# Two attentions by pairs: GpSimdE scales the probabilities, VectorE only inverts their sums

## What is computed

```python
# block 1, branch a (8 heads) and branch b (8 heads on 2 key heads)
ya = moba_attention(qa, ka, heads(av, A_HEADS))
yb = nsa_attention(qb, kc, vc, ks, vs, kw, vw, gb)
#   per head: p = masked_softmax(s, mask); o = gate * (p @ v)   (selected and window parts)
merged = g[:, :, 0] * (ya @ w_up_a) + g[:, :, 1] * (yb @ w_up_b)
x = x + merged @ w_out
# block 2, layer 0
scores = einsum('bkgqd,bksd->bkgqs', q_blk, kt)
p = softmax(scores, axis=-1)
x = x + (p @ v) @ w_o
```

## Time and profile before

| | us |
|---|---|
| median of 3 runs | 1788.64 |
| lowest, highest | 1788.61, 1788.73 |
| the profiled execution | 1788.58 |
| its span | 1786.80 |
| granted TensorE clock, share of full | 0.999 |

### The profile page before, as it was taken

How to read it: one execution, slowest core, us unless ns; L and a number is a source line. 1 busy time by engine, 2 the same in 40 slices (tenths; PEclk the granted TensorE clock), 3 DMA queues, 4 the chain that set the end, 5 groups by cost and what they waited for, 6 DMA issues and landing times.

```text
span 1786.8 us, 30696 instructions
## 1 busy us (share of the span) xinstructions
PE 1752.3 (98%) x10764; PEld 1546.5 (87%) x10764; DVE 1345.2 (75%) x2466; ACT 980.0 (55%) x1679; POOL 500.1 (28%) x245
## 2 busy tenths in 40 slices
PE   8998999999999999999999999999999999999998
PEld 7995899899888888888888888877999988989997
DVE  6757849899767777777777777876579965669974
ACT  5567555479444444444444444666565545556553
POOL 0150166379144444444444444000000000000000
PEclk9999999999999999999999999999999999999999
DMA  7660454601555555555556665644455564535562
GB/s 293 203 232 13 155 189 153 224 25 48 169 185 188 188 190 190 191 191 192 189 193 226 232 223 188 242 142 165 143 193 188 188 196 149 177 129 178 189 196 75
DMA packets 84719, 313.70 MB, mean 176 GB/s; under 512 B 9360, under 2 KB 9488, under 8 KB 83216
## 3 DMA queue, kind: packets, MB, share of 16 engines
q1 hardware_dynamic: 82912, 304.44, 50.4%
q10 hardware_dynamic: 1712, 7.97, 1.3%
HBM read 304.77 MB, written 7.60 MB: 175 GB/s over the span
## 4 chain that ended last, share of the span: by engine, by line
PE 52%; issue 25%; ACT 9%; DVE 7%; DMA 3%; POOL 1%; PEld 1%; ACTq 1%; DVEq 0%; SPq 0%; POOLq 0%; PEldq 0%
PE bank L798 47%; ACT wsplit L1757 6%; PE bank L1249 3%; DMA raw<-expert_u 3%; DVE act_e L2353 2%; DVE wsplit L2347 2%; POOL wsplit L1400 1%; ACT projq L1579 1%; ACT probs L1579 0%; PEld bank L1249 0%; PE bank L843 0%; PE bank L832 0%; DVE wsplit L1891 0%; DVE projq L2106 0%; DVE att L2092 0%
## 5 line engine op out<-in xcount | busy, mean ns | idle before, releaser
L798 PE MATMUL bank<-HT,wsplit 128*128 128x256 f32 (+1 forms) x5056 | 720.0, 301 | 1.3 <-DVE HT L1934 0.9
L798 PEld LDWEIGHTS bank<-HT,wsplit 128*128 128x128 f32 x5056 | 679.3, 189 | 46.5 <-issue 2.6
L1431 POOL TENSOR_TENSOR wsplit<-raw,wsplit 128x1024 fp32r<-128x1024 f32 x111 | 289.6, 2609 | 370.6 <-ACT wsplit L1757 370.6
L2347 DVE TENSOR_TENSOR wsplit<-raw,wsplit 128x1024 fp32r<-128x1024 f32 x127 | 326.3, 2569 | 64.4 <-ACT wsplit L1757 64.3
L798 PE MATMUL bank<-wsplit,wexp 128*128 128x512 f32 x1536 | 373.4, 393 | 0.7 <-DVE wexp L2372 0.6
L798 PEld LDWEIGHTS bank<-wsplit,wexp 128*128 128x128 f32 x1536 | 279.4, 188 | 58.2 <-DVE wsplit L2347 1.9
L1757 ACT ACTIVATE wsplit<-raw 128x1024 fp32r<-128x1024 f32 x238 | 238.3, 1046 | 30.0 <-PE bank L798 26.8
L1765 ACT ACTIVATE act_e<-act_e 128x256 f32<-128x256 f32 x112 | 46.8, 418 | 317.6 <-DVE act_e L2353 317.6
L1466 ACT ACTIVATE wsplit<-raw 128x1024 fp32r<-128x1024 f32 x148 | 156.4, 1059 | 111.5 <-PE bank L798 110.5
L1891 DVE TENSOR_TENSOR wsplit<-raw,wsplit 128x1024 fp32r<-128x1024 f32 x124 | 154.5, 1258 | 78.5 <-ACT wsplit L1466 77.7
L1891 DVE TENSOR_TENSOR wsplit<-raw1b,wsplit 128x1024 fp32r<-128x1024 f32 x102 | 122.6, 1221 | 43.9 <-ACT wsplit L1466 43.5
(11 more groups left out here) (288 smaller groups left out, 2032.9 us busy)
## 6 DMA issues: line engine op xcount, KB each, us to landing
raw<-weights SPq DMA_DIRECT2D x148, 512.0 KB, 4.2
raw<-expert_v SPq DMA_DIRECT2D x127, 512.0 KB, 3.7
raw<-expert_u SPq DMA_DIRECT2D x119, 512.0 KB, 4.4
raw1b<-weights SPq DMA_DIRECT2D x102, 512.0 KB, 4.3
raw1a<-weights SPq DMA_DIRECT2D x48, 512.0 KB, 4.7
early_u<-expert_u SPq DMA_DIRECT2D x5, 512.0 KB, 3.6
raw1a<-expert_u SPq DMA_DIRECT2D x4, 512.0 KB, 3.8
parked<-memT SPq DMA_DIRECT2D x1, 2048.0 KB, 7.3
```

The costliest lines, as they stand in the source:

```text
L798: ins = pe.matmul(out, lhsT, rhs, start=start, stop=stop, **kw)
L1431: pool.tensor_tensor(wsplit[:, s, 1, :], raw0[:, s, :], f32(wsplit[:, s, 0, :]), ALU.subtract).then_inc(u_lo, 1)
L2347: dve.tensor_tensor(wsplit[:, 2 + s, 1, :], src, f32(wsplit[:, 2 + s, 0, :]), ALU.subtract).then_inc(v_lo, 1)
```

## The change

`normalise` is taken from VectorE. There, `invert` makes the inverse and signals a new semaphore `s_inv`; VectorE no longer waits for it. GpSimdE gets a `normalise(use)` that goes through all jobs in order, waits for `s_inv` of the job, makes the same two multiplications in place, and signals `s_prob` as before. It stands in GpSimdE's stream twice: for "ab" after the low part of unit 49, with the last turn of the loop over weight units written out and the units 51, 53 and 55 behind it; for "self" at the very end, after the experts.

```diff
@@ gpsimd
-            with pool.Fori(WIN_END // RAW, OUT0 // RAW) as i:
+            with pool.Fori(WIN_END // RAW, OUT0 // RAW - 1) as i:
                 lo_turn(i, WIN_END, odd)
 
+            def normalise(use):
+
+                jobs, _, Pb, _ = USES[use]
+                for j, job in enumerate(jobs, JOBS[use]):
+                    pool.wait_ge(s_inv, j + 1)
+                    for t in range(T):
+                        r, p = att[:, 2, j % 4, t:t + 1], Pb[:, j % 4, t, 0:seen(use, t)]
+                        if job["gate"] is None:
+                            ins = pool.tensor_scalar(p, p, r, None, ALU.mult)
+                        else:
+                            ins = pool.tensor_scalar(p, p, r, job["gate"](t), ALU.mult, ALU.mult)
+                    ins.then_inc(s_prob, 1)
+
+            lo_turn(OUT0 // RAW - 1, WIN_END, odd[0:1])
+            pool.wait_ge(gate3_done, 1)
+            normalise("ab")
+            lo_turn(OUT0 // RAW - 1, WIN_END, odd[1:])
...
                     pool.wait_ge(u_hi, i * 2 + (s + 1))
                     u_second_part(s)
+            normalise("self")
@@ vector
-                def normalise(step, i):
-
-                    job, j = jobs[2 * step + i], j0 + 2 * step + i
+                def invert(step, i):
+
+                    j = j0 + 2 * step + i
                     dve.wait_ge(s_exp, j + 1)
-                    link(dve.reciprocal(att[:, 2, j % 4, :], att[:, 1, j % 4, :]))
-                    for t in range(T):
-                        r, p = att[:, 2, j % 4, t:t + 1], Pb[:, j % 4, t, 0:seen(use, t)]
-                        if job["gate"] is None:
-                            ins = dve.tensor_scalar(p, p, r, None, ALU.mult)
-                        else:
-                            ins = dve.tensor_scalar(p, p, r, job["gate"](t), ALU.mult, ALU.mult)
-                    ins.then_inc(s_prob, 1)
+                    dve.reciprocal(att[:, 2, j % 4, :], att[:, 1, j % 4, :]).then_inc(s_inv, 1)
...
-                            normalise(step, i)
+                            invert(step, i)
```

More of the change, by code:

```diff
@@ L443, in block_stack @@
         s_full, s_max, s_exp, s_prob = sem("scores_full"), sem("scores_max"), sem("scores_exp"), sem("scores_prob")
+        s_inv = sem("scores_sum_inverted")
         last_gate_full, last_gate_out = sem("last_gate_full"), sem("last_gate_out")
```

## The result

The changed kernel takes **1794.61 us** (median, 1793.84 to 1797.08) against 1788.61 us of the kernel before beside it: ratio **1.0035**, 95% interval 1.0025 to 1.0045, so 6.0 us slower. The forecast was 1801.5 us (+12.9). The sign and the range held; the forecast change was twice the measured one. The profiled execution has a span of 1792.1 us against 1786.8.

A forecast was written before the change was run, and what follows sets the result against it. It took a ScalarE-VectorE latency loop to bound both attentions, with GpSimdE becoming the bound after the change: 1788.58 + 5.0 ("ab") + 7.9 ("self") = 1801.5 us, range 1780 to 1835.

The forecast's parts named there:

- What bounds the kernel before: Attentions "ab" and "self": no engine full, a ScalarE-VectorE latency loop of 3.35 and 3.98 us per pair.
- Rival 1: Both attentions: GpSimdE keeps up, turns shrink to about 2.9 and 3.5 us, gain 6.8 us, 1781.8 us; chance 0.27.
- The price of L1426: GpSimdE's comparison and product, 128 columns: 1.333 us includes a wait for VectorE; 0.84 us is its own work.
- Rival 2: GpSimdE's scalings: L1426's 1.33 us is all own work, "ab" +28.6, "self" +23.6, 1840.8 us; chance 0.13.
- one price for all forms: GpSimdE's scalings: 0.84 us for 128 columns and 1.12 for 256, with one scalar as with two.
- the term +5.0: "ab": 47.0 us of GpSimdE scalings against a 43.0 us stage, last scaling at 188.6 instead of 183.6.
- the sum by throughput: Both attentions: GpSimdE's summed scaling time, 47.0 and 35.8 us, exceeds the stages' 43.0 and 28.1 and sets their ends.
- I add nothing for hunger: GpSimdE in the attentions: four probability buffers let exponentials run two pairs ahead, so no idle time was added.
- The term +7.9: "self": 35.8 us of GpSimdE scalings from 1192.5, ending at 1228.3 instead of 1220.4.
- What would show it: New profile: GpSimdE scalings back to back, almost no idle time; "ab" near 48 us, "self" near 36.
- The odd weight units: Three units queued behind GpSimdE's 48 "ab" scalings: no cost, since GpSimdE is free by 188.6; they started at 192.91 before.
- No switch of routine: Rival 4, before GpSimdE's first scaling: it must switch routine, costing 0 to some us, inside the range.

The follow-up runs named there:

- With two products: The changed kernel with every one-product GpSimdE scaling given a second product by 1.0; 1786.01 us, ratio 0.9981.
- the shared kernel: All GpSimdE scalings written as two products, and VectorE scales each head's first tile, GpSimdE the second; 1784.87 us, ratio 0.9976.

## Why the prediction was right or wrong

- **What bounds the kernel before** was read rightly: a loop of latencies in both stages. With two products the turn of "self" came to 3.63 us where I had 3.5; in "ab" it stayed at 3.39 where I had 2.9. Rival 1's time of 1781.8 was missed mostly for that reason, and not by its price: with prices no higher than its own the kernel takes 1786.0.
- **The price of L1426** of before without its wait, 0.84 us: 0.80 alone, against 1.333 in the row. Rival 2 (1.33 as own work) was rightly put aside.
- **The step that failed first: one price for all forms**, "the same 1.12 us with one scalar" and 0.84 and 1.12 for two. Measured 0.60 and 0.92 for one, 0.45 and 0.56 for two. "ab" needs 8 x (0.60+0.92) + 16 x (0.45+0.56) = 28.3 us of GpSimdE, not 47.0, and the term +5.0 measured +0.05. That it came out so even is luck: GpSimdE was not the bound there, but a loop through it took 6.81 us for two pairs where the exchange of VectorE and ScalarE had taken 6.71. "self" needs 28.9 us, not 35.8. Rival 1 had the two-product price almost exactly (0.46 and 0.74 against 0.45 and 0.56) for the reason it gave, that the comparison is what costs. The page "GPSIMD Engine Reference" of the Trainium skill (section "Engine selection") has one figure for work with one input, roughly line rate. Here the form with two products takes 0.8 ns for each further column and that with one product 2.5, so it cannot hold for both.
- **The step that failed second: the sum by throughput.** "It becomes the bound in both": in neither. With the right price the same sum gives "self" an end at 1192.5+28.9=1221.4, +1.0, and it came 5.5 later: 4.5 us that the sum had at nothing ("I add nothing for hunger"). GpSimdE's gaps between the pairs add up to 5.0 us, and its first scaling began 0.55 sooner. I had said that four buffers feed GpSimdE two pairs ahead; but TensorE issues the scores of a later pair behind the turning that waits for GpSimdE, so no backlog forms after the first two pairs. The term +7.9 is thus +5.5 by two errors of opposite sign: the price 6.9 us too high, the waiting 4.5 us too low. That it looks close is luck.
- **What would show it**: TensorE's turning waits for GpSimdE, as forecast; "almost no idle time before the scalings" was wrong (1.09 and 0.53 us in "self", up to 4.37 in "ab").
- **The odd weight units** cost nothing: L1401 at 192.96, before at 192.91. **No switch of routine** shows before the first scaling (141.58, right behind the weight unit that ends at 141.5). **Both stages in full**: +5.5 at the last scaling of "self", +5.3 in the span. The hop is not 0.04 but 0.08 us (the chain's 1213.31 to 1213.39), once in a loop of 8.85 us, so it is small.

## What to carry to other kernels

Price an instruction by its exact form (operations, scalars, inputs), not by its engine and size: here, at 256 columns, one more product halved its time, and a comparison in the place of the first of two products more than doubled it. When work moves to another engine, do not only add up that engine's busy time; follow a result round the loop through every in-order queue and count how many turns one trip spans. In this kernel 1.2 us of extra work behind the signal lengthened two turns by 0.06 us, and 0.37 us of extra work ahead of it in each turn cost 2 us and more, in part by the clock. The ends of a stage are another matter: there the new engine's work lies on the path with its whole length, here 3.5 of 6.0 us.

## What was not expected of the hardware

- GpSimdE multiplies by one scalar in 0.92 us for 256 columns and by two in 0.55 (0.48 with 1.0 as the second). Why was not found out.
- With a VectorE scaling beside it, GpSimdE's took longer: 637 ns in the shared kernel, where VectorE's starts 0.05 us earlier, against 478 (one product: 1073 against 923). Whether it waits first, as beside an instruction with two inputs, or runs slower, these runs do not tell. Timeline of both there:

```profile
1204.34 0.35 DVE L2124 TENSOR_SCALAR probs<-probs,att 128x256 f32<-128x256 f32 x1
1204.39 0.64 POOL L1425 TENSOR_SCALAR probs<-probs,att 128x256 f32<-128x256 f32 x1 [1.98 <-DVE att L2120]
```

- TensorE's granted clock stood at 1.00 in "self" of the changed kernel, where TensorE waits up to 1.1 us at a time for GpSimdE; with 0.37 us of work added per pair it fell, in the profiled execution, to between 0.60 and 0.72 in five of the seven stretches of 5 us from 1195 to 1230. That execution took 1803.94 us, and the two whose clock hardly fell 1796.59 and 1797.44. Here a small added wait thus went together with a loss of more than its length. What tips it stays open.
